# Attention in a hybrid encoder step: normalised probabilities turned, values stationary for two heads, new keys beside cached ones, one mask and one bias product

## The reference

```python
def fox_attend(q, k, v, cq, ck, qpos, kpos):
    s = jnp.einsum('bqhd,bkhd->bhqk', q, k).astype(jnp.float32) * (FOX_HEAD_DIM ** -0.5)
    s = s + jnp.swapaxes(cq, 1, 2)[:, :, :, None] - jnp.swapaxes(ck, 1, 2)[:, :, None, :]
    s = jnp.where(kpos[None, :] <= qpos[:, None], s, -jnp.inf)
    p = jax.nn.softmax(s, axis=-1).astype(v.dtype)
    return jnp.einsum('bhqk,bkhd->bqhd', p, v)
```

## Time and profile before

| | |
|---|---|
| median of 3 runs | 2037.82 us (2030.97 to 2039.06) |
| the profiled execution | 2038.09 us, of which the span is 2036.2 us |
| TensorE busy | 1921.4 us (94%) |
| VectorE / ScalarE / GpSimd busy | 970.4 / 709.9 / 219.1 us |
| mean granted TensorE clock | 0.963 |

### The profile page before, as it was taken

How to read it: one execution, slowest core, us unless ns; L and a number is a source line. 1 busy time by engine, 2 the same in 40 slices (tenths; PEclk the granted TensorE clock), 3 DMA queues, 4 the chain that set the end, 5 groups by cost and what they waited for, 6 DMA issues and landing times.

```text
span 2036.2 us, 29670 instructions
## 1 busy us (share of the span) xinstructions
PE 1921.4 (94%) x12360; PEld 1738.4 (85%) x12360; DVE 970.4 (48%) x1509; ACT 709.9 (35%) x1119; POOL 219.1 (11%) x358
## 2 busy tenths in 40 slices
PE   5998999999989999899999969999999899999997
PEld 5988879998877887689998869998888788899985
DVE  3355464333455677644333664333543455533433
ACT  3235423333245435233332233333232453333321
POOL 4003200000061213130000100000030130000000
PEclk8899999999989999899999979999989999999998
DMA  6245434443343333254433324433353462444431
GB/s 215 91 145 194 138 115 127 131 126 124 114 146 95 108 117 98 70 157 124 125 126 124 125 93 124 124 125 124 117 187 105 166 203 78 142 127 124 127 128 66
DMA packets 179156, 259.43 MB, mean 127 GB/s; under 512 B 14669, under 2 KB 122333, under 8 KB 179024
## 3 DMA queue, kind: packets, MB, share of 16 engines
q1 hardware_dynamic: 160736, 195.61, 30.1%
q0 software_dynamic: 18288, 61.94, 9.5%
HBM read 243.20 MB, written 13.19 MB: 126 GB/s over the span
## 4 chain that ended last, share of the span: by engine, by line
PE 87%; DVE 6%; ACT 3%; DMA 2%; issue 1%; POOL 1%; SPq 0%; ACTq 0%; DVEq 0%; POOLq 0%
PE ps L1438 15%; PE ps L1439 14%; PE ps L1440 14%; PE ps L1447 10%; PE ps L1449 10%; PE ps L1448 10%; PE ps L1626 1%; PE ps L1702 1%; PE ps L1613 1%; DVE xT_lo L683 1%; DVE x_tok L737 1%; DMA w_raw<-in_w_fox_in_dram 1%; DVE x_tok L722 1%; PE ps L1685 1%; DVE stats L711 1%
## 5 line engine op out<-in xcount | busy, mean ns | idle before, releaser
L664 DVE TENSOR_TENSOR w_lo<-w_raw,w_hi 128x1024 fp32r<-128x1024 f32 x370 | 456.9, 1239 | 813.4 <-ACT w_hi L385 812.9
L385 ACT ACTIVATE w_hi<-w_raw 128x1024 fp32r<-128x1024 f32 x370 | 389.9, 1059 | 922.0 <-DMA w_raw<-in_w_ffn_in_dram 408.3
L1438 PE MATMUL ps<-xT_hi,w_hi 128*128 128x384 f32 x1664 | 570.5, 343 | 23.3 <-DVE xT_lo L683 22.3
L1439 PE MATMUL ps<-xT_lo,w_hi 128*128 128x384 f32 x1664 | 568.7, 342 | 0.0
L1440 PE MATMUL ps<-xT_hi,w_lo 128*128 128x384 f32 x1664 | 568.6, 342 | 0.0
L1438 PEld LDWEIGHTS ps<-xT_hi,w_hi 128*128 128x128 f32 x1664 | 318.8, 192 | 26.3 <-issue 24.6
L1439 PEld LDWEIGHTS ps<-xT_lo,w_hi 128*128 128x128 f32 x1664 | 318.8, 192 | 0.3
L1440 PEld LDWEIGHTS ps<-xT_hi,w_lo 128*128 128x128 f32 x1664 | 318.3, 191 | 0.0
L1449 PE MATMUL ps<-w_hi,hT_lo 128*128 128x512 f32 x528 | 209.6, 397 | 0.0
L1447 PE MATMUL ps<-w_hi,hT_hi 128*128 128x512 f32 x528 | 209.2, 396 | 0.0
L1448 PE MATMUL ps<-w_lo,hT_hi 128*128 128x512 f32 x528 | 207.7, 393 | 0.0
(11 more groups left out here) (295 smaller groups left out, 1995.2 us busy)
## 6 DMA issues: line engine op xcount, KB each, us to landing
w_raw<-in_w_ffn_in_dram SPq DMA_DIRECT2D x352, 256.0 KB, 3.2
w_raw<-in_w_ffn_out_dram SPq DMA_DIRECT2D x176, 256.0 KB, 2.8
w_raw<-in_w_fox_in_dram SPq DMA_DIRECT2D x96, 256.0 KB, 2.9
k_c<-in_cache_fox_k_dram POOLq DMA_DIRECT2D x32, 512.0 KB, 4.7
v_c<-in_cache_fox_v_dram POOLq DMA_DIRECT2D x32, 512.0 KB, 3.8
w_raw<-in_w_hgrn_in_dram SPq DMA_DIRECT2D x64, 256.0 KB, 3.0
w_raw<-in_w_fox_out_dram SPq DMA_DIRECT2D x32, 256.0 KB, 2.7
gb<-in_ln_g_dram POOLq DMA_DIRECT2D x8, 512.0 KB, 4.0
```

The lines of the kernel that those rows point to most:

```text
L385: nc.scalar.activation(w_hi[:, slot, :], w_raw[:, slot, :], ACT.Copy).then_inc(hi_ready, 1)
L664: V.tensor_tensor(w_lo[:, slot, :], w_raw[:, slot, :], w_hi[:, slot, :].bitcast(F32), ALU.subtract).then_inc(lo_ready, 1)
L1438: mm(out, w_hi[:, slot, cols], x_hi[:, k, :], start=k == 0, stop=False)
L1439: mm(out, w_hi[:, slot, cols], x_lo[:, k, :], start=False, stop=False)
```

## The change

- Probabilities of the prompt are divided by their row sums in SBUF, between the exponentials and the transposes (two `tensor_scalar` on `p_p`, new semaphore `scaled`). `p_turn` waits for that.
- `p_out(k)` runs in even turns for two heads at once: the values of a head (64 columns) are stationary, each head on its own half of the array's columns, and the turned probabilities move. The result comes out already turned, so `o_tok`, the `o_ev` reads and `p_heads` go. `pT_p` now lies where `o_tok` was, and ScalarE waits for `kstored`.
- `ktc` has 16 columns more for each strip; VectorE copies the new keys there, and `s_pairs` has four products of 272 columns instead of eight.
- `p_scores` has one bias and one mask product of 384 columns; `c_p` and `causal_r` are widened for it, in five small set-up steps on VectorE and GpSimd.
- The order in a turn changes on three engines: `s_fold`, `p_scores`, `s_turn`, `s_keys`, `p_turn`, `s_out`, `p_out`, `s_pairs` on TensorE. The sample maximum and exponentials come first in the next turn instead of last in this one. The fold writes to bank 2 always, which adds waits on `pT_ev` and `s_lo`.

```diff
-        o_tok = kv_tok[:, 0, 0:2, :]
+        pT_p = kv_tok[:, 0, 0:2, :].rearrange("p a c -> p (a c)")[:, 0:2 * T].rearrange("p (b t) -> p b t", b=2)
...
+                act.wait_ge(*at(f["kstored"], 16 * 2))
                 for n in range(HEADS + 2):
...
                     if n >= 2:
                         m = n - 2
                         act.wait_ge(*at(f["s_xT"], m + 1))
                         nc.scalar.activation(xT_hi[:, 4 * (m % 2):4 * (m % 2) + 4, SEQ + DT * (m // 2):SEQ + DT * (m // 2) + DT],
...
+                                             ps[:, PT_BANK, T:T + 4 * DT].rearrange("p (g q) -> p g q", g=4),
                                              ACT.Copy).then_inc(f["s_hi"][0], 1)
...
+                    if 1 <= n <= HEADS:
+                        act.wait_ge(*at(f["s_nmax"], n))
+                        nc.scalar.activation(p_s[:, (n - 1) % 2, :], ps[:, SS_BANK, 0:PAST + DT], ACT.Exp,
+                                             bias=nmx[:, (n - 1) % 2, 2:3], accum_out=rs[:, (n - 1) % 2, 2:3]).then_inc(f["s_exp"][0], 1)
+                        act.wait_ge(*at(f["s_pT"], n))
+                        nc.scalar.activation(pT_s[:, (n - 1) % 2, :], ps[:, SPT_BANK, 0:T], ACT.Copy).then_inc(f["s_pT_ev"][0], 1)
+                    if n < HEADS:
                         act.wait_ge(*at(f["ktr"], n + 1))
...
+                        nc.scalar.activation(ktc[:, 0:2, 0:PAST], ps[:, KT_BANKS, :].rearrange("p (g s) -> p g s", g=2),
                                              ACT.Copy).then_inc(f["kt_a"][0], 1)
                     if 1 <= n <= HEADS:
...
+                        act.wait_ge(*at(f["pT"], n))
+                        if n >= 3:
+                            act.wait_ge(*at(f["o"], (n - 1) // 2))
+                        nc.scalar.activation(pT_p[:, (n - 1) % 2, :], ps[:, PT_BANK, 0:T], ACT.Copy).then_inc(f["pT_ev"][0], 1)
                     if n < HEADS:
                         act.wait_ge(*at(f["nmax"], n + 1))
                         for q, lo, hi in ((0, 0, P), (1, P, T)):
                             ins = nc.scalar.activation(p_p[:, n % 2, lo:hi], ps[:, S_BANK[n % 2], lo:hi], ACT.Exp,
                                                        bias=nmx[:, n % 2, q:q + 1], accum_out=rs[:, n % 2, q:q + 1])
                         ins.then_inc(f["exp"][0], 1)
...
+                    if n >= 2 and n % 2 == 0:
+                        k = n // 2 - 1
+                        act.wait_ge(*at(f["o"], k + 1))
+                        nc.scalar.activation(xT_hi[:, k, 0:SEQ], ps[:, O_BANK, 0:SEQ], ACT.Copy).then_inc(f["oT_hi"][0], 1)
...
                 for n in range(HEADS + 2):
+                    if 1 <= n <= HEADS:
+                        dve.wait_ge(*at(f["s_scores"], n))
+                        V.tensor_reduce(nmx[:, (n - 1) % 2, 2:3], ps[:, SS_BANK, 0:PAST + DT], AX_X, ALU.max,
+                                        negate=True).then_inc(f["s_nmax"][0], 1)
+                    if n >= 2:
+                        m = n - 2
+                        ks, tt = slice(4 * (m % 2), 4 * (m % 2) + 4), slice(SEQ + DT * (m // 2), SEQ + DT * (m // 2) + DT)
+                        dve.wait_ge(*at(f["s_hi"], m + 1))
+                        V.tensor_tensor(xT_lo[:, ks, tt], ps[:, PT_BANK, T:T + 4 * DT].rearrange("p (g q) -> p g q", g=4),
+                                        xT_hi[:, ks, tt].bitcast(F32), ALU.subtract).then_inc(f["s_lo"][0], 1)
+                    if 1 <= n <= HEADS:
+                        m = (n - 1) % 2
+                        dve.wait_ge(*at(f["exp"], n))
+                        V.reciprocal(rcp[:, m, 0:2], rs[:, m, 0:2]).then_inc(f["rcp"][0], 1)
+                        dve.wait_ge(*at(f["rcp"], n))
+                        for q, lo, hi in ((0, 0, P), (1, P, T)):
+                            ins = V.tensor_scalar(p_p[:, m, lo:hi], p_p[:, m, lo:hi], rcp[:, m, q:q + 1], None, ALU.mult)
+                        ins.then_inc(f["scaled"][0], 1)
+                    if n >= 3 and n % 2:
+                        k = (n - 3) // 2
+                        dve.wait_ge(*at(f["oT_hi"], k + 1))
+                        V.tensor_tensor(xT_lo[:, k, 0:SEQ], ps[:, O_BANK, 0:SEQ], xT_hi[:, k, 0:SEQ].bitcast(F32),
+                                        ALU.subtract).then_inc(f["oT_lo"][0], 1)
                     if n < HEADS:
                         bank = S_BANK[n % 2]
                         dve.wait_ge(*at(f["scores"], n + 1))
                         V.tensor_reduce(nmx[:, n % 2, 0:1], ps[:, bank, 0:P], AX_X, ALU.max, negate=True)
                         V.tensor_reduce(nmx[:, n % 2, 1:2], ps[:, bank, P:T], AX_X, ALU.max,
                                         negate=True).then_inc(f["nmax"][0], 1)
...
+                        now = slice(SEQ + DT * (n // 2), SEQ + DT * (n // 2) + DT)
                         dve.wait_ge(*at(f["ktr"], n + 1))
...
+                        V.tensor_copy(ktc[:, 2:4, 0:PAST], ps[:, KT_BANKS + 1, :].rearrange("p (g s) -> p g s", g=2))
+                        V.tensor_copy(ktc[:, :, PAST:], kT[:, 4 * (n % 2):4 * (n % 2) + 4, now]).then_inc(f["kt_d"][0], 1)
                     if 1 <= n <= HEADS:
                         m = n - 1
...
                         dve.wait_ge(*at(f["s_exp"], m + 1))
...
+                        V.reciprocal(rcp[:, m % 2, 2:3], rs[:, m % 2, 2:3]).then_inc(f["rcs"][0], 1)
+                        dve.wait_ge(*at(f["rcs"], m + 1))
                         dve.wait_ge(*at(f["s_o"], m + 1))
                         V.scalar_tensor_tensor(out=x_s[:, m % 2, :], in0=ps[:, SPT_BANK, T:T + P], scalar=rcp[:, m % 2, 2:3],
                                                in1=own[:, :, :].rearrange("p e d -> p (e d)"), op0=ALU.mult,
                                                op1=ALU.mult).then_inc(f["s_x"][0], 1)
...
                     bank = S_BANK[h % 2]
                     if h >= 2:
                         pe.wait_ge(*at(f["exp"], h - 1))
-                    for lo, hi, off, q in ((0, P, 0, 0), (0, SEQ, P, 1)):
-                        out = ps[:, bank, off:off + hi]
-                        mm(out, sel_p[:, h:h + 1].broadcast_to([CROWS, P]), c_p[:, 0:hi], start=True, stop=False,
-                           skip_group_check=True)
-                        mm(out, qz[:, h % 2, h // 2, q * P:(q + 1) * P], kT[:, h // 2, 0:hi], start=False, stop=False,
-                           skip_group_check=True)
-                        last = mm(ps[:, bank, off + hi - P:off + hi], ident_r[:, :], causal_r[:, :], start=False, stop=True,
-                                  skip_group_check=True)
-                    last.then_inc(f["scores"][0], 1)
+                    out = ps[:, bank, 0:T]
+                    mm(out, sel_p[:, h:h + 1].broadcast_to([CROWS, P]), c_p[:, :], start=True, stop=False, skip_group_check=True)
+                    mm(out, ident_r[:, :], causal_r[:, :], start=False, stop=False, skip_group_check=True)
+                    mm(out[:, 0:P], qz[:, h % 2, h // 2, 0:P], kT[:, h // 2, 0:P], start=False, stop=False, skip_group_check=True)
+                    mm(out[:, P:T], qz[:, h % 2, h // 2, P:SEQ], kT[:, h // 2, 0:SEQ], start=False, stop=True,
+                       skip_group_check=True).then_inc(f["scores"][0], 1)
...
                 def p_turn(h):
-                    pe.wait_ge(*at(f["exp"], h + 1))
+                    pe.wait_ge(*at(f["scaled"], h + 1))
                     if h:
                         pe.wait_ge(*at(f["pT_ev"], h))
+                        pe.wait_ge(*at(f["s_lo"], h))
...
                 def s_fold(n):
                     pe.wait_ge(*at(f["s_x"], n + 1))
-                    pe.wait_ge(*at(f["s_exp"], min(n + 2, 2 * DB)))
-                    mm(ps[:, FOLD_BANK[n], T:T + 4 * DT], x_s[:, n % 2, :], fold[:, :, :].rearrange("p g q -> p (g q)"), start=True,
-                       stop=True).then_inc(f["s_xT"][0], 1)
-
-                def p_heads(k):
-                    pe.wait_ge(*at(f["o_ev"], 2 * k + 2))
-                    for t in range(2):
-                        ins = nc.tensor.transpose(ps[:, O_BANK, P + t * P:P + (t + 1) * P], o_tok[:, t, k * P:(k + 1) * P],
-                                                  ident[:, :])
-                    ins.then_inc(f["oT"][0], 1)
-
...
+                def p_out(k):
+                    pe.wait_ge(*at(f["pT_ev"], 2 * k + 2))
+                    if k:
+                        pe.wait_ge(*at(f["oT_lo"], k))
+                    for a in range(2):
+                        for e in range(2):
+                            h = 2 * k + e
+                            mm_out = ps[HD * e:HD * e + HD, O_BANK, a * P:SEQ]
+                            pT = pT_p[:, e, 2 * P:T] if a else pT_p[:, e, 0:SEQ]
+                            last = mm(mm_out, kv_tok[:, 1, a, HD * h:HD * h + HD], pT, start=a == 0, stop=a == 1,
+                                      skip_group_check=True)
+                    last.then_inc(f["o"][0], 1)
 
```

(26 more changed lines are left out.)

92 lines of the change are left out of this document (22 added, 70 removed).

## The result

The changed kernel takes 2010.03 us (median of 4 runs, 2006.49 to 2013.26) beside 2036.08 us for the kernel before on the same chip (4 runs, 2030.97 to 2039.06): a ratio of 0.987, 95% interval 0.9845 to 0.9904. So it is 22 to 26 us faster, where 11 were forecast and 2018 was the lower end of the range.

What follows compares the result with a forecast made beforehand. TensorE was taken as the bound, with 87% of the chain. Main turns gain 4.4 us, start 0.65, end 0.5: 5.6 a layer, 11.2 for both, so 2037.8 - 11.2 = 2026.6 us; range 2018 to 2038.

Steps and rivals of the forecast that it cites:

- A new wait of 0.2 ahead of `s_turn`: Each attention turn: TensorE's work ends at 1.22 but s_turn waits for the exponentials until 1.42, a 0.2 us wait.
- `p_out`: Even turns: two heads side by side on the array's column halves take 0.65 us, then 0.15 for the width change.
- The slower rival: p_out: the array's halves do not run together, costing 5.2 us a layer or more, 2037 to 2042; chance 0.12.
- The hand-over to `p_out`: Even turns: ScalarE copies pT_p after ktc, so p_out starts 1.35 us after the keys, a new wait of 0.24.
- `s_pairs`: Cached and new keys in merged 272-column products, then the bias: 0.79 us instead of 0.85, bounds 0.69 and 0.85.
- Odd turns: Attention turns without p_out: 4.56 us each, from 2.63 + 1.14 + 0.79.
- Even turns: Attention turns with p_out for two heads: 5.57 us each, from 2.63 + 1.35 + 0.80 + 0.79.
- Start and end: Attention loop outside its thirteen main turns: 0.65 us gained at the start, 0.5 at the end after rounding down.
- beyond it only small set-up work is touched: Everything outside the two attention loops: only small set-up work changes, so the sum held only the loops' 11.2 us.
- Changes of width cheaper: Rival for s_out, p_out and s_pairs: width changes cost less, 8.5 us a layer gained, 2021; chance 0.15.
- VectorE and GpSimd: Rival: the new SBUF multiplies wait for GpSimd's k_c issue in odd turns, costing 3.9 us, 2031; chance 0.13.
- VectorE as the bound: Rival: multiplies and keys' copy reach their upper bounds and beyond, delaying odd turns, some 2033; chance 0.10.

Runs made afterwards that it cites:

- e8_halves_in_turn: The changed kernel with p_out's four products ordered head by head instead of alternating between the array's halves; 2006.63 us in one run, even turns 5.43.
- e7_new_keys_apart: The changed kernel with the new keys as four separate 16-column products again, without VectorE's copy of them; 2005.82 us in one run, turns 5.44 and 4.50.
- e6_pairs_before_out: The changed kernel with s_pairs ahead of p_out in even turns and some ScalarE and VectorE work moved later; 2010.57 us, ratio 0.9867, against the kernel before.
- e12_multiplies_twice: The changed kernel with both VectorE multiplies of the probabilities run twice, first into an unused tile; 2013.6 us in one run, turns 5.42 and 4.53.

## Why the prediction was wrong

**Its own steps in the attention.** Counting as it did, from the moment after the bias product (195.26, where `s_fold` now starts):

- *A new wait of 0.2 ahead of `s_turn`.* Forecast at 1.42, it came at 196.57 - 195.26 = 1.31, since TensorE follows 0.05 us behind ScalarE and not the 0.17 that I took. TensorE's own work ahead of it is 1.24, not 1.22: `p_scores` takes 1.09 (195.41 to 196.07 + 2 x 0.215), not 1.00, and `s_fold` 0.15. So the wait is 0.07. Keys turned at 2.57 instead of 2.63.
- *`s_out`* starts 0.42 after `p_turn`, three transposes at 0.11 and 0.09 for the change of width (0.12 forecast), with no wait: right.
- *`p_out`* 199.86 - 199.06 = 0.80: right, and the halves run together (`e8_halves_in_turn`). The slower rival falls.
- *The hand-over to `p_out`*, 199.06 - 197.83 = 1.23 instead of 1.35. ScalarE and the weight load in the same turn:

```profile
198.03 0.60 ACT L496 ACTIVATE ktc<-ps 128x512 f32<-128x512 f32 x1 [0.38 <-PE ps L1630]
198.52 0.49 ACT L502 ACTIVATE kv_tok<-ps 128x384 f32<-128x384 f32 x1
```
```profile
199.06 0.63 PEld L1670 LDWEIGHTS ps<-kv_tok 128*64 128x64 f32 x8 [0.22 <-ACT kv_tok L502]
```

The copy of `pT_p` ends at 199.01 and TensorE loads weights at 199.06: 0.05 where I took 0.16. The row that I took it from had the product 0.14 behind the copy, and its weight load 0.11; why TensorE goes on sooner here is open.
- *`s_pairs`* 0.60 + 0.23 = 0.83 instead of 0.79; by `e7_new_keys_apart` the merging gains nothing. Its bound of 0.85 was the better reading.
- *Odd turns* 4.53 (4.56 forecast): right. *Even turns* 5.42 (5.57): 0.15 too long, the keys' 0.06 and the hand-over's 0.12 less `s_pairs`' 0.04. Main part 65.2 (66.4 forecast).
- *Start and end.* Turn 1 shortens by 0.7 to 0.85 (0.65 forecast), and from the last `p_scores` to the output product behind the last `s_fold` 13.79 us become 12.97: 0.8 instead of the 0.5 that I had left "after rounding down". Of these, 0.66 lie ahead of the first output product, and the two transposes of the last `p_heads`, which I had left out, are the rest.

Together 7.2 us a layer instead of 5.6. The term that was off is the hand-over from ScalarE, 0.11 too long wherever TensorE waits for it, and with it the end; the others are small and lie on both sides. That the total of the attention came out 3 us short is thus a matter of sizes: its order and its overlaps were right, and its two new waits are there, 0.1 us each instead of 0.2.

**The step that failed** is the one ahead of the sum: "beyond it only small set-up work is touched". By it every layer outside the attention entered the sum with a difference of nothing. The change takes 438 records out of TensorE's stream ahead of the recurrent layer, and by that moves every place there at which a block of 256 ends. Where 91 unused transposes put those places back, the change is worth 0.9937, 12.8 us (8.7 to 16.7) of 2032.4, which agrees with the attention's 14.4; the 7 to 10 us between that kernel's 2019.2 and the 2009.4 to 2012.0 of the others go with where the blocks end. That much is shown by moving them; by what path the blocks cost all of it is open (above). The rows lay in that very layer, and the waits put down to "issue" stood in the same trace; I read neither for what they say about the program as a whole.

**The rivals.** *Changes of width cheaper* gave 2021, nearest to the result, for a reason that is not so: the changes cost about what was forecast (0.09 of 0.12 ahead of `s_out`, 0.15 of 0.15 behind `p_out`), and `e6_pairs_before_out` and `e7_new_keys_apart` show them taking up whatever is saved beside them. Its 8.5 us a layer does not follow from its turns of 5.3 and 4.5 either: these give 6.7 for the main part and, with the start and the end, 7.9. *VectorE and GpSimd* do meet, in the even turns and not the odd ones:

```profile
196.22 0.76 DVE L873 TENSOR_SCALAR p_p<-p_p,rcp 128x128 f32<-128x128 f32 x2
```
```profile
196.12 0.74 POOL L1140 DMA_DIRECT2D k_c<-in_cache_fox_k_dram  x1
```

The pair takes 0.76 instead of 0.55, and ends at 196.98, 0.12 behind GpSimd's issue. That costs nothing in a turn whose `p_out` waits for ScalarE. Of the lock that the Trainium skill describes (SBUF — State Buffer, "Who interferes with whom") the trace shows half: the second multiply is held until GpSimd is done, the first, begun inside the same issue, takes its usual 0.29. In three turns of layer 3 (from 1622.50, 1632.45 and 1652.37) the first multiply began 0.03 to 0.09 us ahead of the issue, and the second, inside the issue, was not held either (0.35), nor was the issue longer (0.73). *VectorE as the bound* falls with `e12_multiplies_twice`.

**The chances.** Faster by over 0.5% had 0.45, and no case reached below 2018, since all cases varied the same two loops.

## What to carry to other kernels

Read the waits of the bounding engine that are put down to "issue", in every layer, and number that engine's instructions: where it works off some 256 of them in two or three microseconds, the place at which a block ends is a cost that any edit far away can move, here by 5 us in one kernel and 7 to 10 in the other. Count a stop only for what it adds to the idle time of the whole layer: it can take the place of a wait behind it. To judge an edit, compare kernels whose later layers stand alike (a few unused instructions in an early wait set this right), or give the forecast a term of its own for it. And take the gain of a changed order from the turn: once the queues are full, a merged product or a hidden wait gives back in changes of width what it saves.
